# Writing the low half of each weight chunk over its own staging slot, and letting TensorE's use free the slot

## The chip, the cores and the metric

One core of a Trainium2 chip runs the whole program. The metric is the device time of one execution, in microseconds (us). Three runs of the kernel before gave a median of 2979.61 us, the lowest 2978.82 and the highest 2984.75.

## What is computed

The reference is a stack of transformer blocks on 256 tokens of width 1024, in float32. Two layers of a first block come first, each with a gated feed-forward network (FFN, inner width 2816), a mixer of three attention branches, and a second such FFN. Two layers of a second block follow, each with an attention and a mixture of 16 experts of which every token takes two. Every layer modulates its input with vectors computed from a conditioning vector `c`:

```python
c_act = jax.nn.silu(c)
for l in range(DEPTH):
    mod = (c_act @ ada_w[l] + ada_b[l]).reshape(bsz, N_SUB, 3, D_MODEL)[:, :, :, None, :]
    h = modulate(x, norm_pre[l, 0], mod[:, 0, 0], mod[:, 0, 1])
    x = residual_add(x, swiglu(h, ffn_w_gate[l, 0], ffn_w_up[l, 0], ffn_w_down[l, 0]), norm_post[l, 0], mod[:, 0, 2], 0.5)
    ...
```

The product `c_act @ ada_w` is a vector times a very wide matrix. The kernel calls this the modulation, and reads its weights (`ada_stream`) in slices.

## The kernel before

**Weights.** All weights of the matrix products are one stream of 432 chunks of 128 partitions x 2048 float32 (1 MB each), in the order in which TensorE uses them. To keep float32 accuracy, a weight chunk is split into a high half in a rounded type (`w_hi`) and the rest (`w_lo`). Each product is then three matmuls (`mm3`, L1564 to L1571): high by high, high by low, low by high. Three engines and a queue work on a chunk in turn:

- SyncE (the SP queue) loads chunk n into staging slot n mod 6 (`chunk`, L392). It first waits until the low half of chunk n-6 has been written, by the semaphore `chunk_ready`, because VectorE's subtraction is the last reader of the slot.
- ScalarE copies the slot to `w_hi`, buffer n mod 3 (`hi`, L504). It waits for the landing and for TensorE to have finished chunk n-3 (`pe_used`).
- VectorE subtracts, `w_lo` = `stage` - `w_hi`, into a low buffer of its own, n mod 3 (`lo`, L876), and raises `chunk_ready`.
- TensorE waits for `chunk_ready` (`chunk_wait`, L1573), does its matmuls and raises `pe_used`. That semaphore starts at 3 (`PARTS`), so the value n+1 says that chunk n-3 is finished.

**Modulation.** The modulation weights are cut into 40 units of 4 slices (768 KB a slice, one buffer for each of the four slice numbers). SP loads a slice (`ada_slice`, L399) after VectorE has used up the same slice of the unit before. VectorE multiplies and adds each slice in two steps (`ada_add`, L949 to L967, 8 steps a unit), and TensorE then sums the unit over partitions (`sum_unit`, L1642 to L1650). Four units are done at the start of the program, and nine in each of the four dense FFNs (33 chunks each, starting at chunks 0, 71, 104 and 175).

**The dense FFN's block.** An FFN has 11 blocks of 3 chunks. In block g TensorE does chunk 3g-1 (up), a transpose of the hidden values, the sum of a modulation unit, chunk 3g (up), chunk 3g+1 (down). Chunk 3g-1 also waits for `silu(g-1)` of VectorE, which frees the result banks `gu`. VectorE's order in block g is written out by hand (L1036 to L1057); `add` is `ada_add` of the unit of block g:

```python
add(0)
lo(n0 + 3 * g - 1, i)
add(1)
silu(g - 1, i)
add(2)
lo(n0 + 3 * g, i)
...
```

It goes on with add 3, `lo` of chunk 3g+1, add 4, `turn_lo(g-1)`, which the down chunk 3g+1 needs, and adds 5 to 7. Steps 0, 2, 4 and 6 are each the first use of a slice.

**SP's order.** SP executes its waits and issues in program order. In the FFN's loop, chunks and slices are interleaved (L434 to L439):

```python
for a in range(2):
    for q in range(SLICES):
        if q < 3:
            chunk(n0 + 12 + 3 * a + q, i)
        ada_slice(unit_base[k] + 1 + a, q, i)
```

Counted in blocks: slices 0, 1 and 2 of block g's unit stand right behind chunks 3g+3, 3g+4 and 3g+5, and slice 3 behind slice 2. This holds for g = 3 to 10. The four slices of block 2's unit are issued before, in one go.

**The mixture of experts** uses 96 chunks in each of its two layers, with 12 matmuls of 128 x 512 a chunk, where a dense chunk has 24. It loads no slices.

Of the kernel before, what the change touches and what calls it, by code (L numbers as in the profile page):

```python
# [2 lines left out]

# [4 lines left out]
F32 = mybir.dt.float32  # L28
# [6 lines left out]
P = 128  # L35
# [19 lines left out]
CW = 2048  # L55
# [171 lines left out]
def build(nc, wstream, ada_stream, xin, const_in, vec_in, bgate_in, lam_in, rbias_in, t5_in, t5hot_in, rel_in, rw_in, out):  # L227
# [8 lines left out]
    with ExitStack() as ctx:  # L236
# [4 lines left out]
            return ctx.enter_context(nc.semaphore(name))  # L241


        stage = sb("stage", [P, STAGES, CW])
        w_hi = sb("w_hi", [P, PARTS, CW], F32R)
        w_lo = sb("w_lo", [P, PARTS, CW], F32R)

        x = sb("x_tok", [P, NT, D])
        tok = sb("tok", [P, NT, D])
# [140 lines left out]
        @block.sync  # L390
        def _(sp):
            def chunk(n, i=0, rounds=1):  # L392
                if not isinstance(i, int) or n >= STAGES:

                    sp.wait_ge(chunk_ready, n + 1 - STAGES + STAGES * rounds * i)
                at = bass.ds(n + STAGES * rounds * i, 1)
                sp.dma_start(stage[:, n % STAGES, :], wstream[at].rearrange("a p c -> (a p) c")).then_inc(
                    landed[n % STAGES], 16)

            def ada_slice(unit, q, i=0):  # L400

                m = SLICES * unit + q
                if not isinstance(i, int) or m >= SLICES:
                    sp.wait_ge(slice_sum, m + 1 - SLICES + 2 * SLICES * i)
                at = bass.ds(m + 2 * SLICES * i, 1)
                sp.dma_start(ada_stage[:, q, :], ada_stream[at].rearrange("a p c -> (a p) c")).then_inc(
                    ada_landed[q], 16)

            def stream(n, end):

                turns = (end - n) // STAGES
                if turns > 1:
                    with sp.Fori(0, turns) as i:
                        for s in range(STAGES):
                            chunk(n + s, i)
                    n += turns * STAGES
                for m in range(n, end):
                    chunk(m)

            for unit in range(FIRST_UNITS + 1):  # L420
                for q in range(SLICES):
                    ada_slice(unit, q)
                    if unit >= FIRST_UNITS - 1 and q % 4 < 3:
                        chunk(3 * (unit - FIRST_UNITS + 1) + q)
            n = STAGES
            for k, n0 in dense_steps:
                stream(n, n0 + 8)
                if k:

                    sp.wait_ge(x_ready, NT * k)  # L430
                    for q in range(SLICES):
                        ada_slice(unit_base[k], q)
                stream(n0 + 8, n0 + 12)
                with sp.Fori(0, (FFN_UNITS - 1) // 2) as i:  # L434
# [5 lines that stand above are left out]
                n = n0 + 12 + 3 * (FFN_UNITS - 1)  # L440
            stream(n, n_chunks)
            sp.wait_ge(x_ready, NT * NSUB)
            sp.dma_start(out.rearrange("(t p) d -> p t d", p=P), x[:]).then_inc(st_out, 16)
            sp.wait_ge(st_out, 16)
# [420 lines left out]
        def _(dve):  # L865
# [10 lines left out]
            def lo(n, i=0, rounds=1):  # L876

                dve.wait_ge(hi_ready, n + 1 + STAGES * rounds * i)
                dve.tensor_tensor(w_lo[:, n % PARTS, :], stage[:, n % STAGES, :], w_hi[:, n % PARTS, :].bitcast(F32),  # L879
                                  ALU.subtract).then_inc(chunk_ready, 1)  # L880

            def ahead(n):
# [681 lines left out]
        def _(pe):  # L1564
# [11 lines left out]
            def columns(n, dst, k0, kts, first, last, width=512, src=(hT_hi, hT_lo), i=0, pitch=512):  # L1576

                chunk_wait(n, i)
                s = n % PARTS
                for t in range(NT):  # L1580
                    for k in range(kts):
                        c = slice(k * pitch, k * pitch + width)
                        lhs = [v[:, k0 + k, t * P:(t + 1) * P] for v in src]
                        ins = mm3(dst(t), lhs[0], lhs[1], w_hi[:, s, c], w_lo[:, s, c], first and k == 0, last and k == kts - 1)
                ins.then_inc(pe_used, 1)

            def rows(n, lhs, first, last, i=0, rounds=1):

                chunk_wait(n, i, rounds)
                s = n % PARTS  # L1590
                for t in range(NT):
                    for k in range(2):
                        l_hi, l_lo = lhs(k, t)
                        for h in range(2):
                            c = slice(k * D + h * 512, k * D + (h + 1) * 512)
                            ins = mm3(acc[:, 2 * t + h, :], l_hi, l_lo, w_hi[:, s, c], w_lo[:, s, c],
                                      first and k == 0, last and k == 1)
                    if last and t == 0:
                        ins.then_inc(half_done, 1)
                ins.then_inc(pe_used, 1)  # L1600
# [73 lines left out]
            def moe(b, l):  # L1674
# [39 lines left out]
                def up(e, j, half, i=0):  # L1714
                    p, n = e // 2, moe_up_at(n0, e, j) + half
                    if half == 0:
                        if e % 2 == 0 and j == 0:
                            taken(("g", p, KT - 1), i)
                        if not isinstance(i, int) or e:
                            pe.wait_ge(hid_ready, g0 + 2 * e + j - 1 + 8 * i)  # L1720
                    chunk_wait(n, i, 4)
                    slots = slice((e % 2) * P, (e % 2 + 1) * P)
                    src_hi, src_lo = gathered[p % 2]
                    for k in range(4):
                        c = slice(k * 512, (k + 1) * 512)
                        ins = mm3(gu[:, j, :], src_hi[:, 4 * half + k, slots], src_lo[:, 4 * half + k, slots],
                                  w_hi[:, n % PARTS, c], w_lo[:, n % PARTS, c], half == 0 and k == 0, half == 1 and k == 3)
                    ins.then_inc(pe_used, 1)

                def turn_hidden(e, i=0):  # L1730
# [6 lines left out]
                def down(e, h, i=0):  # L1737

                    if h == 0:
                        taken(("hid", e), i)  # L1740
                    n = moe_down_at(n0, e, h)
                    dst = bank(("y", e, h), i)
                    chunk_wait(n, i, 4)
                    for k in range(4):
                        c = slice(k * 512, (k + 1) * 512)
                        ins = mm3(dst, hid_hi[:, k * P:(k + 1) * P], hid_lo[:, k * P:(k + 1) * P],
                                  w_hi[:, n % PARTS, c], w_lo[:, n % PARTS, c], k == 0, k == 3,
                                  signal=pe_used if h and k == 0 else None)
                    ins.then_inc(tr_full, 1)

# [61 lines left out]
            def moe_dense(b):  # L1812
# [14 lines left out]
                def down(e, h, i=0):  # L1827
# [5 lines left out]
                    for t in range(NT):  # L1833
                        for k in range(4):
                            c = slice(k * 512, (k + 1) * 512)
                            ins = mm3(acc[:, 2 * t + h, :], yT_hi[:, k, t * P:(t + 1) * P], yT_lo[:, k, t * P:(t + 1) * P],
                                      w_hi[:, n % PARTS, c], w_lo[:, n % PARTS, c], first and k == 0, last and k == 3)
                        if last and h == 1 and t == 0:
                            ins.then_inc(half_done, 1)
                    ins.then_inc(pe_used, 1)  # L1840
# [49 lines left out]
            for step, b in plan:  # L1890
# [150 lines left out]
                elif kind == "mla_up":  # L2041
# [2 lines left out]
                    pe.wait_ge(o_free, b["ov"])  # L2044
                    wide = acc[:].rearrange("p (t a) c -> p t a c", t=NT)
                    chunk_wait(n)
                    s = n % PARTS
                    for t in range(NT):
                        for h, w in ((0, 512), (1, 256)):
                            for k in range(2):  # L2050
                                c = slice(k * 768 + h * 512, k * 768 + h * 512 + w)
                                ins = mm3(wide[:, t, h, 0:w], yT_hi[:, k, t * P:(t + 1) * P], yT_lo[:, k, t * P:(t + 1) * P],
                                          w_hi[:, s, c], w_lo[:, s, c], k == 0, k == 1)
                    ins.then_inc(pe_used, 1)
                    chunk_wait(n + 1)
                    s = (n + 1) % PARTS
                    pe.wait_ge(ev_ready, b["ev"] + 1)
                    for t in range(NT):
                        for h in range(2):
                            c = slice(h * 512, h * 512 + 512)  # L2060
                            ins = mm3(wide[:, t, h, :], yT_hi[:, 2, t * P:(t + 1) * P], yT_lo[:, 2, t * P:(t + 1) * P],
                                      w_hi[:, s, c], w_lo[:, s, c], True, True)
                    ins.then_inc(pe_used, 1)
                elif kind == "merge":
                    pe.wait_ge(o_free, b["ov"])
# [222 lines left out]
```

## Time and profile before

| what | value |
|---|---|
| median of three runs | 2979.61 us |
| the profiled execution: span from first to last instruction | 2981.6 us |
| TensorE (PE) busy | 2593.6 us, 87% |
| VectorE (DVE) busy | 1984.8 us, 67% |
| ScalarE (ACT) busy | 1269.8 us, 43% |
| mean granted clock of TensorE | 0.892 |
| DMA | 591.74 MB, mean 198 GB/s |

The profile gives the time of each instruction group, who ended an engine's idle time, and the granted clock as a share of 2.4 GHz (1.00 or 0.50). The span of the profiled execution is 2.0 us over the median of the runs; the profile has no other time for that execution than this span, so sums below are made against 2981.6 us and put on the median.

### The profile page before, as it was taken

The numbers are of one execution on the slowest core, as the hardware profiler recorded it, in microseconds if no ns is written. First come the engines' busy times: TensorE is split into PE (matmuls) and PEld (weight loads), VectorE is DVE, ScalarE is ACT, GpSimd is POOL, SyncE is SP. The second block draws the span as 40 slices with busy tenths as digits, with TensorE's granted clock in tenths as the row PEclk, the third lists the DMA queues.
The fourth block names the chain that finished last, engine by engine and source line by source line (L and its number), as shares of the span: only waits on it lengthen the run. The fifth ranks groups of instructions, "written<-read, shape, count | busy, mean of one in ns | idle before, by whom it ended". The sixth has DMA issues, their size and how long they took to land.

```text
span 2981.6 us, 33031 instructions
## 1 busy us (share of the span) xinstructions
PE 2593.6 (87%) x11582; PEld 2113.7 (71%) x11582; DVE 1984.8 (67%) x2444; ACT 1269.8 (43%) x1403; POOL 98.0 (3%) x136
## 2 busy tenths in 40 slices
PE   2998976988998999769989988689999779799997
PEld 2787865866877877658768875478887557578885
DVE  6687354556876874445668856678887444588885
ACT  1333443433333334444333342256666322366663
POOL 1000000000000000000000002000000021000000
PEclk9999956998998999668989998899999785899998
DMA  9585400445875864103458743147777333177773
GB/s 358 231 350 222 169 29 29 162 168 204 357 284 215 356 275 155 43 29 131 151 199 340 315 155 78 57 180 285 269 284 278 136 106 27 65 288 276 276 290 116
DMA packets 89959, 591.74 MB, mean 198 GB/s; under 512 B 10616, under 2 KB 10632, under 8 KB 34432
## 3 DMA queue, kind: packets, MB, share of 16 engines
q1 hardware_dynamic: 85520, 579.90, 50.9%
q0 software_dynamic: 2608, 7.31, 2.0%
q10 hardware_dynamic: 1728, 3.15, 0.4%
q8 instruction: 66, 1.08, 0.1%
q14 instruction: 37, 0.30, 0.0%
HBM read 589.25 MB, written 1.06 MB: 198 GB/s over the span
## 4 chain that ended last, share of the span: by engine, by line
PE 77%; DVE 11%; ACT 5%; issue 3%; POOL 2%; DMA 1%; DVEq 0%; ACTq 0%; POOLq 0%
PE gu L1567 11%; PE gu L1570 11%; PE gu L1571 11%; PE acc L1567 7%; PE acc L1570 7%; PE acc L1571 7%; PE tr L1611 4%; PE gu L1865 4%; DVE w_lo L879 3%; PE acc L1865 2%; PE tr L1567 2%; PE tr L1570 2%; PE tr L1571 2%; PE tr L1696 2%; PE tr L1648 1%
## 5 line engine op out<-in xcount | busy, mean ns | idle before, releaser
L879 DVE TENSOR_TENSOR w_lo<-stage,w_hi 128x2048 fp32r<-128x2048 f32 x432 | 984.6, 2287 | 216.9 <-ACT w_hi L508 216.5
L508 ACT ACTIVATE w_hi<-stage 128x2048 fp32r<-128x2048 f32 x432 | 824.4, 1913 | 408.8 <-PE acc L1571 249.5
L1567 PE MATMUL gu<-w_hi,hT_hi 128*128 128x512 f32 x1152 | 466.2, 405 | 19.1 <-DVE pair L1017 14.3
L1570 PE MATMUL gu<-w_lo,hT_hi 128*128 128x512 f32 x1152 | 458.2, 398 | 0.0
L1571 PE MATMUL gu<-w_hi,hT_lo 128*128 128x512 f32 x1152 | 457.3, 397 | 0.0
L966 DVE SCALAR_TENSOR_TENSOR qk<-proj,c_unit,qk 128x768 f32<-128x768 f32 x280 | 284.0, 1014 | 19.7 <-DMA proj<-ada_stream 8.4
L1567 PEld LDWEIGHTS gu<-w_hi,hT_hi 128*128 128x128 f32 x1152 | 222.5, 193 | 67.7 <-DVE pair L1017 17.6
L1571 PEld LDWEIGHTS gu<-w_hi,hT_lo 128*128 128x128 f32 x1152 | 221.7, 192 | 48.4
L1570 PEld LDWEIGHTS gu<-w_lo,hT_hi 128*128 128x128 f32 x1152 | 222.4, 193 | 43.1
L1567 PE MATMUL acc<-w_hi,hT_hi 128*128 128x512 f32 (+1 forms) x544 | 219.0, 402 | 17.0 <-DVE w_lo L879 12.3
L1570 PE MATMUL acc<-w_lo,hT_hi 128*128 128x512 f32 (+1 forms) x544 | 216.9, 399 | 0.0
L1571 PE MATMUL acc<-w_hi,hT_lo 128*128 128x512 f32 (+1 forms) x544 | 215.9, 397 | 0.0
L1567 PE MATMUL acc<-w_hi,yT_hi 128*128 128x512 f32 x472 | 185.2, 392 | 8.5 <-DVE yT_lo L897 4.5
L1611 PE MATMUL tr<-const,tok 128*128 128x128 f32 x336 | 87.5, 421 | 118.7 <-DVE tok L1241 78.3
L1570 PE MATMUL acc<-w_lo,yT_hi 128*128 128x512 f32 x472 | 184.1, 390 | 0.0
L1571 PE MATMUL acc<-w_hi,yT_lo 128*128 128x512 f32 x472 | 184.0, 390 | 0.0
L1611 PEld LDWEIGHTS tr<-const,tok 128*128 128x128 f32 x336 | 63.2, 217 | 148.6 <-DVE tok L1241 82.1
L706 ACT ACTIVATE tok<-tok,nmax 128x128 f32<-128x128 f32 (+1 forms) x128 | 57.1, 447 | 234.5 <-DVE nmax L1209 233.1
L1567 PEld LDWEIGHTS acc<-w_hi,hT_hi 128*128 128x128 f32 x544 | 106.5, 196 | 43.1 <-issue 15.5
L1865 PE MATMUL gu<-qk 64*128 64x128 f32 (+3 forms) x320 | 117.8, 510 | 11.8 <-DVE qk L1320 4.9
L1571 PEld LDWEIGHTS acc<-w_hi,hT_lo 128*128 128x128 f32 x544 | 106.0, 195 | 21.9
L1567 PE MATMUL tr<-w_hi,yT_hi 128*128 128x512 f32 x256 | 104.2, 407 | 19.6 <-DVE w_lo L879 19.6
(233 smaller groups left out, 3724.9 us busy)
## 6 DMA issues: line engine op xcount, KB each, us to landing
stage<-wstream SPq DMA_DIRECT2D x432, 1024.0 KB, 4.8
proj<-ada_stream SPq DMA_DIRECT2D x160, 768.0 KB, 7.6
tf<-bgate_in ACTq DMA_DIRECT2D x12, 256.0 KB, 3.2
proj<-rel_in POOLq DMA_DIRECT2D x16, 128.0 KB, 4.0
const<-const_in POOLq DMA_DIRECT2D x1, 1028.0 KB, 10.6
x_tok<-x_in POOLq DMA_DIRECT2D x1, 1024.0 KB, 14.2
proj<-t_rows POOLq DMA_DIRECT2D x8, 128.0 KB, 4.0
proj<-rel_in POOLq DMA_DIRECT2D x16, 64.0 KB, 3.5
```

Source lines behind the costliest of these rows:

```text
L508: act.activation(w_hi[:, n % PARTS, :], stage[:, n % STAGES, :], ACT.Copy).then_inc(hi_ready, 1)
L706: ins = act.activation(prob[:, s, lo:lo + w], prob[:, s, lo:lo + w], ACT.Exp, bias=nmax[:, s, q:q + 1], accum_out=rsum[:, s, q:q + 1])
L879: dve.tensor_tensor(w_lo[:, n % PARTS, :], stage[:, n % STAGES, :], w_hi[:, n % PARTS, :].bitcast(F32), ALU.subtract).then_inc(chunk_ready, 1)
L966: ins = dve.scalar_tensor_tensor(total, w, c, total, ALU.mult, ALU.add)
L1567: ins = pe.matmul(dst, l_hi, r_hi, start=start, stop=False, skip_group_check=True)
L1570: pe.matmul(dst, l_hi, r_lo, start=False, stop=False, skip_group_check=True)
L1571: return pe.matmul(dst, l_lo, r_hi, start=False, stop=stop, skip_group_check=True)
L1611: ins = pe.transpose(tr[0:rows_, u % 2, j * P:(j + 1) * P], src, ident)
L1648: ins = pe.matmul(tr[:, u % 2, j:j + 1], ada_acc[:, unit % 2, j * P:(j + 1) * P], ones[:, 0:1], start=True, stop=True)
L1696: ins = pe.matmul(dst[:, part * S:(part + 1) * S], h[:, t, r * P:(r + 1) * P], pick[:, t, :], start=(t == 0), stop=(t == NT - 1), skip_gro ...
L1865: return pe.matmul(dst, lhs, rhs, start=start, stop=stop, skip_group_check=True)
```

## The change

The separate tile `w_lo` goes. The name now stands for the staging tile itself, at the same address, in the rounded type, with 6 slots. VectorE's subtraction reads a slot and writes its result over it. TensorE reads the low half from slot n mod 6, so the slot is in use until TensorE has finished the chunk. SP therefore waits on `pe_used` for chunk n-6, where it waited on `chunk_ready` for chunk n-6. The 24 KB per partition of the three low buffers are left unused. Nothing else is changed: the orders of all engines, the three high buffers and all other waits stay.

```diff
+        stage_at = (nc.sbuf_base + 31) // 32 * 32
         stage = sb("stage", [P, STAGES, CW])
         w_hi = sb("w_hi", [P, PARTS, CW], F32R)
-        w_lo = sb("w_lo", [P, PARTS, CW], F32R)
+        w_lo = nc.alloc_sbuf_tensor_at("w_lo", [P, STAGES, CW], F32R, offset=stage_at)
...
             def chunk(n, i=0, rounds=1):
                 if not isinstance(i, int) or n >= STAGES:
 
-                    sp.wait_ge(chunk_ready, n + 1 - STAGES + STAGES * rounds * i)
+                    sp.wait_ge(pe_used, n + 1 - STAGES + PARTS + STAGES * rounds * i)
...
             def lo(n, i=0, rounds=1):
 
                 dve.wait_ge(hi_ready, n + 1 + STAGES * rounds * i)
-                dve.tensor_tensor(w_lo[:, n % PARTS, :], stage[:, n % STAGES, :], w_hi[:, n % PARTS, :].bitcast(F32),
+                dve.tensor_tensor(w_lo[:, n % STAGES, :], stage[:, n % STAGES, :], w_hi[:, n % PARTS, :].bitcast(F32),
                                   ALU.subtract).then_inc(chunk_ready, 1)
...
                 chunk_wait(n, i)
-                s = n % PARTS
+                s, z = n % PARTS, n % STAGES
...
-                        ins = mm3(dst(t), lhs[0], lhs[1], w_hi[:, s, c], w_lo[:, s, c], first and k == 0, last and k == kts - 1)
+                        ins = mm3(dst(t), lhs[0], lhs[1], w_hi[:, s, c], w_lo[:, z, c], first and k == 0, last and k == kts - 1)
```

The other places where TensorE reads `w_lo` change in the same way.

## Rows read from the trace of the kernel before

**Rows 1.** The page's chain that ended last, and its costliest groups

```profile
PE 77%; DVE 11%; ACT 5%; issue 3%; POOL 2%; DMA 1%; DVEq 0%; ACTq 0%; POOLq 0%
...
L879 DVE TENSOR_TENSOR w_lo<-stage,w_hi 128x2048 fp32r<-128x2048 f32 x432 | 984.6, 2287 | 216.9 <-ACT w_hi L508 216.5
```

**Rows 2.** Windows: one dense FFN block, and 338 us of the first mixture of experts

```profile
core 0: us, PE busy (x) PEld busy (x) DVE busy (x) ACT busy (x) POOL busy (x), PEclk, DMA share, GB/s
...
155.60:173.70 18.10, 18.10 (x90) 15.22 (x89) 15.30 (x15) 6.73 (x5) 0.00 (x0) 1.00 0.88 356
...
1962.00:2300.00 338.00, 327.30 (x1582) 270.65 (x1580) 281.19 (x288) 221.51 (x223) 0.00 (x0) 0.99 0.75 280
```

**Rows 3.** Waits of the SP queue: who was waited for, total us, times, longest us

```profile
SPq L397 <- DVE w_lo L879: 2524.0, 426, 116.1
```

**Rows 4.** Timeline of SP: chunks 21 to 23 and the slices of block 6

```profile
162.75 0.33 SPq L397 DMA_DIRECT2D stage<-wstream  x1
163.27 0.33 SPq L406 DMA_DIRECT2D proj<-ada_stream  x1
166.94 0.33 SPq L397 DMA_DIRECT2D stage<-wstream  x1
167.50 0.33 SPq L406 DMA_DIRECT2D proj<-ada_stream  x1
176.37 0.33 SPq L397 DMA_DIRECT2D stage<-wstream  x1
176.91 0.86 SPq L406 DMA_DIRECT2D proj<-ada_stream  x2
```

**Rows 5.** Timeline of VectorE, block 6, from add 0 to turn_lo

```profile
160.29 2.29 DVE L879 TENSOR_TENSOR w_lo<-stage,w_hi 128x2048 fp32r<-128x2048 f32 x1
...
173.26 0.62 DVE L964 TENSOR_SCALAR qk<-proj,c_unit 128x768 f32<-128x768 f32 x1 [0.21 <-DVE qk L966]
173.79 2.29 DVE L879 TENSOR_TENSOR w_lo<-stage,w_hi 128x2048 fp32r<-128x2048 f32 x1
176.00 1.01 DVE L966 SCALAR_TENSOR_TENSOR qk<-proj,c_unit,qk 128x768 f32<-128x768 f32 x1
176.92 0.68 DVE L1017 TENSOR_TENSOR pair<-pair,gu 128x512 f32<-128x512 f32 x1
...
184.81 1.01 DVE L966 SCALAR_TENSOR_TENSOR qk<-proj,c_unit,qk 128x768 f32<-128x768 f32 x1
187.16 0.69 DVE L1022 TENSOR_TENSOR yT_lo<-tr,yT_hi 128x512 fp32r<-128x512 f32 x1 [1.34 <-ACT yT_hi L582]
```

**Rows 6.** Timeline of ScalarE: steps that start as TensorE ends chunks 13, 15, 16

```profile
162.52 1.92 ACT L508 ACTIVATE w_hi<-stage 128x2048 fp32r<-128x2048 f32 x1 [2.96 <-PE acc L1571]
168.40 0.60 ACT L582 ACTIVATE yT_hi<-tr 128x512 fp32r<-128x512 f32 x1 [3.96 <-PE tr L1611]
...
175.28 0.60 ACT L570 ACTIVATE pair<-gu 128x512 f32<-128x512 f32 x1 [4.49 <-PE gu L1571]
...
180.65 1.92 ACT L508 ACTIVATE w_hi<-stage 128x2048 fp32r<-128x2048 f32 x1 [2.95 <-PE acc L1571]
```

**Rows 7.** DMA issues of the page: count, KB each, median us to landing

```profile
stage<-wstream SPq DMA_DIRECT2D x432, 1024.0 KB, 4.8
proj<-ada_stream SPq DMA_DIRECT2D x160, 768.0 KB, 7.6
```

**Rows 8.** Timeline of TensorE, after 3.58 us of idle in the first FFN

```profile
89.45 0.79 PE L1567 MATMUL gu<-w_hi,hT_hi 128*128 128x512 f32 x1 [3.58 <-DVE pair L1017]
90.04 0.63 PE L1570 MATMUL gu<-w_lo,hT_hi 128*128 128x512 f32 x1
90.46 0.63 PE L1571 MATMUL gu<-w_hi,hT_lo 128*128 128x512 f32 x1
...
96.51 0.39 PE L1567 MATMUL gu<-w_hi,hT_hi 128*128 128x512 f32 x1
96.74 0.39 PE L1570 MATMUL gu<-w_lo,hT_hi 128*128 128x512 f32 x1
```

**Rows 9.** Window of the low clock around that restart

```profile
88.80:95.60 6.80, 6.15 (x15) 4.80 (x16) 5.00 (x3) 0.00 (x0) 0.00 (x0) 0.50 0.81 292
```

More of the change, by code:

```diff
@@ L1589, in rows @@
                 chunk_wait(n, i, rounds)
-                s = n % PARTS
+                s, z = n % PARTS, n % STAGES
                 for t in range(NT):
@@ L1595, in rows @@
                             c = slice(k * D + h * 512, k * D + (h + 1) * 512)
-                            ins = mm3(acc[:, 2 * t + h, :], l_hi, l_lo, w_hi[:, s, c], w_lo[:, s, c],
+                            ins = mm3(acc[:, 2 * t + h, :], l_hi, l_lo, w_hi[:, s, c], w_lo[:, z, c],
                                       first and k == 0, last and k == 1)
@@ L1726, in up @@
                         ins = mm3(gu[:, j, :], src_hi[:, 4 * half + k, slots], src_lo[:, 4 * half + k, slots],
-                                  w_hi[:, n % PARTS, c], w_lo[:, n % PARTS, c], half == 0 and k == 0, half == 1 and k == 3)
+                                  w_hi[:, n % PARTS, c], w_lo[:, n % STAGES, c], half == 0 and k == 0, half == 1 and k == 3)
                     ins.then_inc(pe_used, 1)
@@ L1746, in down @@
                         ins = mm3(dst, hid_hi[:, k * P:(k + 1) * P], hid_lo[:, k * P:(k + 1) * P],
-                                  w_hi[:, n % PARTS, c], w_lo[:, n % PARTS, c], k == 0, k == 3,
+                                  w_hi[:, n % PARTS, c], w_lo[:, n % STAGES, c], k == 0, k == 3,
                                   signal=pe_used if h and k == 0 else None)
@@ L1836, in down @@
                             ins = mm3(acc[:, 2 * t + h, :], yT_hi[:, k, t * P:(t + 1) * P], yT_lo[:, k, t * P:(t + 1) * P],
-                                      w_hi[:, n % PARTS, c], w_lo[:, n % PARTS, c], first and k == 0, last and k == 3)
+                                      w_hi[:, n % PARTS, c], w_lo[:, n % STAGES, c], first and k == 0, last and k == 3)
                         if last and h == 1 and t == 0:
@@ L2046, in _ @@
                     chunk_wait(n)
-                    s = n % PARTS
+                    s, z = n % PARTS, n % STAGES
                     for t in range(NT):
@@ L2052, in _ @@
                                 ins = mm3(wide[:, t, h, 0:w], yT_hi[:, k, t * P:(t + 1) * P], yT_lo[:, k, t * P:(t + 1) * P],
-                                          w_hi[:, s, c], w_lo[:, s, c], k == 0, k == 1)
+                                          w_hi[:, s, c], w_lo[:, z, c], k == 0, k == 1)
                     ins.then_inc(pe_used, 1)
                     chunk_wait(n + 1)
-                    s = (n + 1) % PARTS
+                    s, z = (n + 1) % PARTS, (n + 1) % STAGES
                     pe.wait_ge(ev_ready, b["ev"] + 1)
@@ L2061, in _ @@
                             ins = mm3(wide[:, t, h, :], yT_hi[:, 2, t * P:(t + 1) * P], yT_lo[:, 2, t * P:(t + 1) * P],
-                                      w_hi[:, s, c], w_lo[:, s, c], True, True)
+                                      w_hi[:, s, c], w_lo[:, z, c], True, True)
                     ins.then_inc(pe_used, 1)
```

## The prediction

> **What bounds the kernel now.** I read the chain of waits first: TensorE holds 77% of it, VectorE 11%, and DMA 1% [rows 1]. Staging is not a limit. Over the 432 chunks SP waits 2524 us for the low halves [rows 3]: it is always ahead. The windows show what TensorE's neighbours have to spare. A block of a dense FFN takes 18.10 us, TensorE is busy in all of them, VectorE in 15.30, and DMA moves 356 GB/s at a busy share of 0.88 [rows 2]. So there TensorE is the bound, but slices and chunks flow with little slack. I then followed one block on the four timelines, because SP's queue carries two streams and the change alters the wait of only one of them.
>
> **The subtraction in place.** All 432 subtractions stay, with the same operands and sizes, 2287 ns each [rows 1]. I take 0 for the new destination. No row has one in place. If the write over a source made each 1% faster or slower, that would be 10 us of VectorE, on the chain for 11% of its length, so 1 us either way. TensorE reads the same number of values from another address: 0 as well. Removing the three low buffers gives nothing, because nobody waited for them separately: the high buffer's wait for chunk n-3 covers both, and stays.
>
> **The chunk's own load.** A slot now comes free when TensorE ends chunk n-6, not when chunk n-6 has been subtracted. ScalarE's copy of chunk n waits in any case for the end of chunk n-3. The load thus has at least the time of three chunks on TensorE. Matmuls follow each other every 0.23 us [rows 8], so this is 3 x 24 x 0.23 = 16.6 us in dense parts and 3 x 12 x 0.23 = 8.3 us in the experts, against 0.2 us until the issue and 4.8 us to the landing [rows 7]. In the experts the mean is 338 / 92 = 3.7 us a chunk, 11.0 us for three (92 subtractions lie in the window of rows 2). Landings up to 8 us are hidden. I take 0 there too. In the attention stages two fewer chunks are prefetched. Six slots stay full, which is 6 x 24 x 0.23 = 33 us of TensorE work, and the loads that follow start one per chunk used.
>
> **What stands behind the chunk in SP's queue** is where the time goes. In block 6 slice 0 of the modulation stands behind chunk 21, and chunk 21 waits for chunk 15. Before, the subtraction of chunk 15 ended at 160.29 + 2.29 = 162.6, chunk 21 was issued at 162.75 and the slice at 163.27 [rows 4, 5]. VectorE began to use it at 173.26 [rows 5], 10.0 us after the issue, of which the median landing takes 7.6 [rows 7]. After the change the issue waits for the end of chunk 15 on TensorE, which is 175.28 [rows 6]. That is 12.5 us later, and 2 us past the moment of use. VectorE is in order: behind `add(0)` stand the subtraction of chunk 17 and `silu`, both of which TensorE needs for chunk 17.
>
> The late slice now closes a loop through TensorE, so I work out its period, from the start s of chunk 3g-1 to the start of chunk 3g+2:
>
> - s to the end of chunk 3g: chunk 15 ended 12.76 us after chunk 13 (175.28 - 162.52, [rows 6]), with the transpose and the unit's sum in between: 12.8.
> - End of chunk 3g to the issue of slice 0: 0.15 for the chunk (162.75 - 162.6) and 0.5 for the slice [rows 4, 5]: 0.7.
> - Issue to landing: the median is 7.6 [rows 7], with other transfers queued ahead. The DMA will be less crowded. A 1 MB chunk alone takes 4.8. At 356 / 0.88 = 405 GB/s a chunk needs 2.6 us of transfer and a slice 1.9. So a slice issued 0.5 behind a lone chunk lands after 4.8 + 1.9 - 0.5 = 6.2. I take 6.2, with 7.6 as the other end.
> - Landing to the next start: from `add(0)` at 173.26 to the end of `silu` at 177.60 [rows 5], and 0.2 for two semaphores: 4.5.
>
> The sum is 24.2 us, where the block took 18.1: 6.1 more. Part of it is taken inside the block. Slice 2 is issued at the end of chunk 3g-1, 5.4 after s; it lands at 5.4 + 0.7 + 6.2 = 12.3; then add 4 (1.0) and `turn_lo` (0.7) end at 14.2, and the down chunk that waited for them could have begun at 12.8. TensorE thus idles 1.4 us before the down chunk and 4.7 us before chunk 3g+2. This second stall does not lengthen the loop, except once at the FFN's end.
>
> Blocks 3 to 10 are concerned, 8 in each of 4 FFNs. The first loses less, some 5 us, since the block before still ran at the old pace. Per FFN: 5 + 7 x 6.1 + 1.4 = 49; for four FFNs 196 us. The four slices of block 2 stay early: they stand behind the FFN's chunk 7, which waits for chunk 1, and are used after three more chunks, over 16 us later.
>
> **TensorE's clock** adds to that. Before, it was granted 1.00 throughout the blocks [rows 2]. After an idle of 3.58 us matmuls followed each other every 0.43 us instead of 0.23, and the granted clock stood at 0.50 (1.2 GHz) in a window of 6.8 us [rows 8, 9]. About 14 matmuls were slow: 14 x 0.20 = 2.8 us lost. A stall of 4.7 us is longer than that one, so I expect the low clock in most blocks. The lost time lies between s and the end of chunk 3g, so it lengthens the loop in full. Its ends are 0 and 2.8 us a block; I take 2.4, near the only row that has such a stall: 32 x 2.4 = 77 us.
>
> The Trainium skill ("TensorE: Matmul & The Clock Gate", section "HAM oscillation — how this bites in real kernels") describes this pattern: a loop whose matmuls stop for a DMA in each turn starts every turn at the low clock. By that rule every block pays, and the sum is that of the rival "every block cold". The one stall of this trace agrees with it.
>
> **Sum.** 196 + 77 = 273 us over the profiled execution's 2981.6. The median of the runs is 2.0 us less, so I put it on 2979.6: **3253 us**. A difference of 0.2%, 6 us, is about what a measurement of this kernel tells from no change.
>
> **The rivals.**
> - *Every block cold, or crowded landings* (0.2). The low clock costs its full 2.8 us or more in each of the 32 blocks, 196 + 90, or slices take 7.6 us: 31 x 1.4 = 43 us on top. Together 3310. For it: the median of rows 7. Against it: the lighter DMA load of a longer block.
> - *The clock stays up* (0.2). The stall is cut in two and the clock holds: 2980 + 196 = 3176. For it: TensorE is fully busy around the stalls. Against it: rows 8 and 9.
> - *The experts pay as well* (0.05). VectorE is busy for 281 of 338 us there [rows 2], and a load that lands late stops ScalarE, VectorE and TensorE in turn. If each of the 192 chunks lost 0.5 us, it would be 96 us more: 3350. It needs landings above 8 us; the median is 4.8.
> - *The slices come in time: not slower* (0.03). The slack of a slice before was 10.0 - 7.6 = 2.4 us. If SP was held back by less than this, every block would keep 18.1 us and the time would be 2980. It decides at a delay of 2.4 us; rows 4 to 6 show 12.5.
>
> The change surely does what it says: every chunk's wait is replaced.
>
> **How the numbers follow.** The forecast case (low clock in most blocks) has 0.52 and goes from 3200 to 3290. Adding the case of the clock that stays up takes the range down to 3160, the cold and crowded case takes it up to 3330. What is left out are the last two rivals and the tails. Slower by over 0.2%: 0.96; within 0.2%: 0.03; faster: 0.01, for a gain of the writes in place that no row shows.
>
> **What would show it.** In the windows of a dense FFN the block's period is 26 to 27 us instead of 18.1, with VectorE's 15.3 us of work unchanged and DMA down to about 240 GB/s. `add(0)` of VectorE (L964) has idle time ended by DMA `proj<-ada_stream`, about 8 us in a block, where before there was 0.2. TensorE's idle before chunk 3g-1 is ended by `pair` L1017, and the granted clock drops in most blocks. SP waits for PE, not for `w_lo`. The experts take the same 338 us, the attention stages the same time, and L879 the same 2287 ns. The prediction is wrong if slices are used without a wait, if the clock stays at 1.00, or if the time outside the dense FFNs changes by more than 10 us.

## The result, and the profile after

The changed kernel took 3263.99 us (median of 4 runs, 3259.84 to 3272.76), the kernel before 2981.16 us beside it. The ratio is 1.094, with a 95% interval from 1.092 to 1.097. The span of the profiled execution is 3261.9 us, 280.3 more than before. Line numbers of the changed kernel are 19 lower than before: L397 is L378, L406 is L387, L879 is L860, L966 is L947.

The page of the changed kernel: the chain that ended last, and the two groups of VectorE's that matter.

```profile
PE 66%; DVE 13%; DMA 8%; issue 6%; ACT 5%; POOL 1%; SPq 1%; DVEq 0%; ACTq 0%; POOLq 0%
...
L860 DVE TENSOR_TENSOR w_lo<-stage,w_hi 128x2048 fp32r<-128x2048 f32 x432 | 984.5, 2287 | 181.2 <-ACT w_hi L489 180.7
...
L947 DVE SCALAR_TENSOR_TENSOR qk<-proj,c_unit,qk 128x768 f32<-128x768 f32 x280 | 284.4, 1016 | 299.9 <-DMA proj<-ada_stream 288.8
```

DMA went from 1% of the chain to 8%, all of it the slices' landing. VectorE waited 288.8 us for slices in L947, and 107.9 us more in L945, which is `add(0)`. The subtraction costs the same 2287 ns as in [rows 1]: writing in place is free.

The windows of the changed kernel, one dense block and then the first and second experts' stages from the end of their first chunk to the end of their last:

```profile
core 0: us, PE busy (x) PEld busy (x) DVE busy (x) ACT busy (x) POOL busy (x), PEclk, DMA share, GB/s
...
209.90:237.10 27.20, 21.37 (x88) 17.00 (x88) 15.21 (x15) 6.88 (x6) 0.00 (x0) 0.87 0.60 231
...
2246.70:2639.50 392.80, 357.07 (x1681) 293.12 (x1681) 308.96 (x314) 237.36 (x240) 2.39 (x4) 0.96 0.70 257
2884.80:3250.40 365.60, 344.04 (x1634) 283.59 (x1633) 288.70 (x291) 226.73 (x229) 0.00 (x0) 0.98 0.70 258
```

The block that took 18.10 us [rows 2] takes 27.2. VectorE's work in it is the same, 15.2 us, and DMA is down to 231 GB/s. The same stages of the experts took 392.7 and 365.8 us before:

```profile
1963.20:2355.90 392.70, 356.93 (x1681) 293.02 (x1680) 308.93 (x314) 237.51 (x240) 2.40 (x4) 0.96 0.69 257
2604.40:2970.20 365.80, 344.21 (x1634) 283.62 (x1633) 288.68 (x291) 226.91 (x229) 0.00 (x0) 0.98 0.68 253
```

Their 192 chunks lost nothing. Where the difference lies, by the ends of TensorE's chunks: from the end of the first to the end of the last chunk, each dense FFN took 200.1 us before, and 271.8, 274.3, 273.5 and 273.6 us after. That is 1093.2 against 800.4, 293 more. All the rest of the program is 12.5 us shorter (280.3 - 292.8).

More than half of the 12.5 us lies right behind the four FFNs, from the end of their last chunk to the end of the next chunk of the stream: 21.7 to 21.8 us before, 19.9 after, 7.4 in all. The windows of the first, in the kernel before and in the changed kernel:

```profile
278.90:300.70 21.80, 11.68 (x42) 9.17 (x43) 15.35 (x21) 7.71 (x11) 3.71 (x7) 0.69 0.23 89
```

```profile
353.20:373.10 19.90, 9.56 (x41) 7.77 (x42) 15.27 (x21) 7.75 (x11) 3.73 (x7) 0.74 0.13 53
```

TensorE idles 8.76 us there before and 8.74 after, then does transposes and the next chunk. That chunk began with matmuls 0.43 us apart before and 0.23 us apart after: the clock was back at 1.00 earlier in the changed kernel. The attentions of the second block gave 3.6 and 3.3 us (more on them at e9 to e11), and the program's first chunk ended 2.7 us later.

One turn of the loop, on three engines. The first is SP, from the end of chunk 13 on. It issues chunks 19 to 21, with slices 1 to 3 of block 5's unit and slice 0 of block 6's:

```profile
184.40 0.33 SPq L378 DMA_DIRECT2D stage<-wstream  x1
184.99 0.33 SPq L387 DMA_DIRECT2D proj<-ada_stream  x1
194.69 0.33 SPq L378 DMA_DIRECT2D stage<-wstream  x1
195.28 0.86 SPq L387 DMA_DIRECT2D proj<-ada_stream  x2
201.93 0.33 SPq L378 DMA_DIRECT2D stage<-wstream  x1
202.46 0.33 SPq L387 DMA_DIRECT2D proj<-ada_stream  x1
```

Then VectorE, which uses those slices:

```profile
191.23 1.02 DVE L947 SCALAR_TENSOR_TENSOR qk<-proj,c_unit,qk 128x768 f32<-128x768 f32 x1 [4.18 <-DMA proj<-ada_stream]
...
201.54 1.02 DVE L947 SCALAR_TENSOR_TENSOR qk<-proj,c_unit,qk 128x768 f32<-128x768 f32 x1 [3.96 <-DMA proj<-ada_stream]
202.48 0.68 DVE L1003 TENSOR_TENSOR yT_lo<-tr,yT_hi 128x512 fp32r<-128x512 f32 x1
...
208.69 0.62 DVE L945 TENSOR_SCALAR qk<-proj,c_unit 128x768 f32<-128x768 f32 x1 [2.21 <-DMA proj<-ada_stream]
209.23 2.28 DVE L860 TENSOR_TENSOR w_lo<-stage,w_hi 128x2048 fp32r<-128x2048 f32 x1
211.43 1.01 DVE L947 SCALAR_TENSOR_TENSOR qk<-proj,c_unit,qk 128x768 f32<-128x768 f32 x1
212.36 0.68 DVE L998 TENSOR_TENSOR pair<-pair,gu 128x512 f32<-128x512 f32 x1
```

And TensorE's restart one block later:

```profile
240.51 0.79 PE L1548 MATMUL gu<-w_hi,hT_hi 128*128 128x512 f32 x1 [4.44 <-DVE pair L998]
...
241.95 0.63 PE L1548 MATMUL gu<-w_hi,hT_hi 128*128 128x512 f32 x1
...
243.23 0.63 PE L1548 MATMUL gu<-w_hi,hT_hi 128*128 128x512 f32 x1
...
246.66 0.40 PE L1548 MATMUL gu<-w_hi,hT_hi 128*128 128x512 f32 x1
...
247.35 0.39 PE L1548 MATMUL gu<-w_hi,hT_hi 128*128 128x512 f32 x1
```

Slice 0 of block 6's unit is issued at 202.46, right behind chunk 21, which waited for TensorE, and VectorE starts on it at 208.69, 6.2 us later. The end of `silu` is at 213.04. One block later TensorE restarts after 4.44 us of idle, with matmuls of one kind 1.28 us apart (241.95 to 243.23) where at full clock they are 0.69 apart (246.66 to 247.35; every third matmul stands here). In [rows 4, 5] the same slice had waited for VectorE; now VectorE waits for it, and for the slices of L947 too.

### The profile page after: what moved, and what is told of

It is laid out like the page before. It is cut to its first block, busy times and chain, and to the rows that moved or that the text cites. A ratio compares the mean times of both kernels' runs of the same rounds, so it can differ in the third digit from the quotient of the medians.

```text
span 3261.9 us, 32833 instructions
## 1 busy us (share of the span) xinstructions
PE 2675.4 (82%) x11582; PEld 2154.7 (66%) x11582; DVE 1983.7 (61%) x2444; ACT 1268.8 (39%) x1403; POOL 97.8 (3%) x136
## 4 chain that ended last, share of the span: by engine, by line
PE 66%; DVE 13%; DMA 8%; issue 6%; ACT 5%; POOL 1%; SPq 1%; DVEq 0%; ACTq 0%; POOLq 0%
PE gu L1548 11%; PE gu L1551 10%; PE gu L1552 10%; DMA proj<-ada_stream 8%; PE acc L1548 5%; PE acc L1551 5%; PE acc L1552 5%; PE tr L1592 4%; DVE w_lo L860 3%; PE gu L1846 3%; PE acc L1846 2%; PE tr L1548 2%; PE tr L1551 2%; PE tr L1552 2%; DVE qk L947 1%
## 5 line engine op out<-in xcount | busy, mean ns | idle before, releaser
L860 DVE TENSOR_TENSOR w_lo<-stage,w_hi 128x2048 fp32r<-128x2048 f32 x432 | 984.5, 2287 | 181.2 <-ACT w_hi L489 180.7
L1548 PE MATMUL gu<-w_hi,hT_hi 128*128 128x512 f32 x1152 | 498.7, 433 | 167.2 <-DVE pair L998 162.0
L1551 PE MATMUL gu<-w_lo,hT_hi 128*128 128x512 f32 x1152 | 484.4, 420 | 0.0
L1552 PE MATMUL gu<-w_hi,hT_lo 128*128 128x512 f32 x1152 | 481.5, 418 | 0.0
L947 DVE SCALAR_TENSOR_TENSOR qk<-proj,c_unit,qk 128x768 f32<-128x768 f32 x280 | 284.4, 1016 | 299.9 <-DMA proj<-ada_stream 288.8
L1548 PEld LDWEIGHTS gu<-w_hi,hT_hi 128*128 128x128 f32 x1152 | 239.8, 208 | 234.2 <-issue 161.0
L1552 PEld LDWEIGHTS gu<-w_hi,hT_lo 128*128 128x128 f32 x1152 | 237.0, 206 | 55.1
L1551 PEld LDWEIGHTS gu<-w_lo,hT_hi 128*128 128x128 f32 x1152 | 239.2, 208 | 47.5
L1548 PE MATMUL acc<-w_hi,hT_hi 128*128 128x512 f32 (+1 forms) x544 | 216.8, 399 | 17.4 <-DVE w_lo L860 12.3
L563 ACT ACTIVATE yT_hi<-tr 128x512 fp32r<-128x512 f32 x44 | 26.3, 597 | 428.7 <-PE tr L1592 428.7
L1548 PEld LDWEIGHTS acc<-w_hi,yT_hi 128*128 128x128 f32 x472 | 91.1, 193 | 93.3 <-issue 69.0
## 6 DMA issues: line engine op xcount, KB each, us to landing
x_tok<-x_in POOLq DMA_DIRECT2D x1, 1024.0 KB, 15.2
```

The source lines that it names most:

```text
L563: act.activation(hid_hi, tr[:, u % 2, :], ACT.Copy).then_inc(th_ready, 1)
L860: dve.tensor_tensor(w_lo[:, n % STAGES, :], stage[:, n % STAGES, :], w_hi[:, n % PARTS, :].bitcast(F32), ALU.subtract).then_inc(chunk_read ...
L947: ins = dve.scalar_tensor_tensor(total, w, c, total, ALU.mult, ALU.add)
L1548: ins = pe.matmul(dst, l_hi, r_hi, start=start, stop=False, skip_group_check=True)
L1551: pe.matmul(dst, l_hi, r_lo, start=False, stop=False, skip_group_check=True)
L1552: return pe.matmul(dst, l_lo, r_hi, start=False, stop=stop, skip_group_check=True)
```

## The experiments

All are short edits of one of the two kernels. "Early" is this edit of SP's order, which puts a slice behind a chunk that is three places ahead in the stream:

```diff
-                stream(n0 + 8, n0 + 12)
+                stream(n0 + 8, n0 + 9)
...
-                                chunk(n0 + 12 + 3 * a + q, i)
+                                chunk(n0 + 9 + 3 * a + q, i)
...
-                n = n0 + 12 + 3 * (FFN_UNITS - 1)
+                n = n0 + 9 + 3 * (FFN_UNITS - 1)
```

| run | kernel | median us | ratio to before, 95% interval |
|---|---|---|---|
| changed | in place, wait for TensorE | 3263.99 | 1.092 to 1.097 |
| e1 | changed, early | 2975.32 | 0.9956 to 0.9979 |
| e2 | before, wait for TensorE | 3263.52 | 1.092 to 1.097 |
| e3 | before, wait for TensorE outside the loop | 2990.50 | 1.0014 to 1.0043 |
| e4 | changed, slices one chunk earlier | 2975.55 | 0.9961 to 0.9989 |
| e5 | changed, filler matmuls | 3220.38 | 1.076 to 1.083 |
| e6 | e1 with six high buffers | 2954.64 | 0.9904 to 0.9938 |
| e7 | before, early | 2984.19 | 1.0003 to 1.0033 |
| e8 | changed, slices issued by GpSimd | 2975.83 | 0.9981 to 1.0000 |
| e9 | e2, early | 2975.74 | 0.9959 to 0.9985 |
| e10 | e7 again | 2985.86 | 0.9989 to 1.0019 |
| e11 | e1 again | 2975.38 | 0.9953 to 0.9977 |

The kernel before had medians of 2982.38 us beside e1 to e4, 2979.69 beside e5 to e8 and 2982.92 beside e9 to e11.

**e1: the changed kernel with the slices early.** What was expected:

> The changed kernel, with the slices of a modulation unit standing one group of three chunks earlier in SP's queue (slice 0 of block g's unit behind chunk 3g, not 3g+3). The low half stays in place and every chunk still waits for TensorE. Theory (the loss is the slices' wait behind a chunk in SP's queue): a slice is then issued at least 12 us before VectorE needs it, the block takes 18.1 us and the time is 2981, within 10. Rival A (the shared slot or the write in place is slow by itself): 3264, unchanged. Rival B (two fewer chunks are loaded ahead, and that starves TensorE): 3264 or close to it, as the chunks' own issues don't move.

Measured: 2975.32 us. Both rivals fall. The low half still lies in the staging slot and every chunk still waits for TensorE, so neither the shared slot nor the shorter prefetch costs time. One block in the windows of e1, and VectorE's first use of a slice in it:

```profile
156.40:174.50 18.10, 18.10 (x89) 15.24 (x88) 15.36 (x14) 6.73 (x5) 0.00 (x0) 1.00 0.98 373
```

```profile
174.57 0.62 DVE L945 TENSOR_SCALAR qk<-proj,c_unit 128x768 f32<-128x768 f32 x1 [0.22 <-DVE qk L947]
```

The block is back at 18.10 us and VectorE no longer waits for a DMA.

**e2: the wait alone, in the kernel before.**

```diff
-                    sp.wait_ge(chunk_ready, n + 1 - STAGES + STAGES * rounds * i)
+                    sp.wait_ge(pe_used, n + 1 - STAGES + PARTS + STAGES * rounds * i)
```

> The kernel before with one edit: SP waits for TensorE's end of chunk n-6 instead of the subtraction of chunk n-6. The low half keeps its three buffers of its own. Theory: 3264, within 5, as the wait is the whole loss. Rival A (write in place or shared slot): 2981.

Measured: 3263.52 us, 0.5 from the changed kernel. The wait is the whole loss and the write in place has no part in it.

**e3: the wait everywhere but in the loop.**

```diff
+                    if loop:
+                        sp.wait_ge(chunk_ready, n + 1 - STAGES + STAGES * rounds * i)
+                    else:
+                        sp.wait_ge(pe_used, n + 1 - STAGES + PARTS + STAGES * rounds * i)
```

> The kernel before, with SP's wait for TensorE on all chunks except the 24 chunks of each dense FFN's loop among which the slices stand (those wait for the subtraction, as before; low halves in buffers of their own). Theory: 336 of 432 chunks wait for TensorE and nothing is lost: 2981, within 6. Rival B (fewer chunks ahead costs everywhere, the experts above all): 3000 to 3100.

Measured: 2990.50 us, 8 over the 2982.38 beside it; the expectation of 2981 within 6 missed. Rival B's low end of 3000 is not reached. The trace tells where the 8 come from. Each FFN took 204.4 to 204.9 us instead of 200.1, 18 in all, while the blocks in mid-loop took the usual 18.1 us. The rest of the program was 11 us shorter. At an FFN's start chunk n0+11 stands ahead of the loop in SP's queue and waits for TensorE here, and slice 0 of block 3 stands two issues behind it: it went out at 116.73 us in e3 and at 109.56 before. VectorE's first use of that slice in e3, whose line numbers are 3 higher than before:

```profile
124.83 0.62 DVE L967 TENSOR_SCALAR qk<-proj,c_unit 128x768 f32<-128x768 f32 x1 [4.57 <-DMA proj<-ada_stream]
```

One late slice per FFN, 4.57 us: the mechanism of the loop, once. In the experts, where 192 chunks wait for TensorE, the two stages took 392.7 and 365.7 us.

**e4: the slices one chunk earlier.** In the changed kernel the numbers 9 of the early edit are 11.

> The changed kernel with the slices only one chunk earlier in SP's queue (slice 0 of block g's unit behind chunk 3g+2). By the theory's loop slice 0 is issued when chunk 3g-4 ends, 7.2 us earlier than in the changed kernel (one chunk of 5.4 us, the transpose and the sum), the loop closes in 24.2 - 7.2 = 17.0 us, under the 18.1 us that TensorE needs, and the stall before the down chunk goes as slice 2 comes 5.4 us earlier: 2985, from 2980 to 3000. Were the loss only proportional to the delay (10 us of 12.5), a third to a half of it would stay: 3080 to 3160.

Measured: 2975.55 us, under the 2980 to 3000 that was expected. In the medians, moving the slices by one chunk in SP's queue takes away as much as moving them by three. In the profiled execution the FFNs still took 201.6 to 203.6 us, 9 more in sum than in e1, in the first three turns of the loop (up to 20.6 us); the later turns took 18.1 to 18.3. The loss is not proportional to the delay: it is there when the loop through SP, DMA, VectorE and TensorE is longer than TensorE's own work, and all but gone when it is shorter. The end of chunk 3g-4 took the place of the end of chunk 3g-3 in it.

**e5: filler matmuls in the stall.**

```diff
                     down(n0 + 3 * g + 1, g - 1, isinstance(i, int) and g == 1, False, i)
+                    if g >= 2:
+                        for _ in range(18):
+                            pe.matmul(tr[:, u_of(g - 1) % 2, :], hT_hi[:, 0, 0:P],
+                                      hT_hi[:, 0:2, :].rearrange("p a s -> p (a s)"), start=True, stop=True)
```

> The changed kernel plus 18 matmuls of 128x512 without use in every dense FFN block from the second on, right behind the down chunk, where TensorE idles some 4.5 us (40 blocks in all, of which 36 lie in blocks 3 to 10 or close to them; 18 x 0.23 = 4.1 us each). They write a bank that is free there and change no result. Theory (part of the loss is the low clock after each stall): the clock stays at 1.00 in the loop, the block falls from 27.0 to 24.5 us, and the time is 3264 - 32 x 2.5 = 3184, from 3175 to 3205, although work was added. Rival (the low clock lies off the loop, or the stall is not idle time that can be filled): 3264 or more, up to 3264 + 36 x 4.1 = 3410.

Measured: 3220.38 us. The kernel does 648 more matmuls and is 44 us faster than the changed kernel, where the rival had it slower. Two of its blocks in the windows:

```profile
175.00:199.90 24.90, 22.80 (x106) 18.47 (x106) 14.87 (x14) 5.64 (x6) 0.00 (x0) 1.00 0.63 247
199.90:224.80 24.90, 22.80 (x106) 18.47 (x106) 15.70 (x16) 7.31 (x6) 0.00 (x0) 1.00 0.67 255
```

In these two blocks the granted clock stands at 1.00 and the block at 24.9 us, 2.3 under the changed kernel's 27.2. Over the last seven turns of all four FFNs the mean is 25.0 us against 27.2; the first turn or two of each FFN still had some low clock. The expectation of 3184 (3175 to 3205) missed, by my count of the fillers. Seven periods per FFN lie between two stalls, which gives 7 x 2.2 = 15 us; the filler of block 10 has no stall to fill and adds 4.1. That leaves 11 per FFN, and the FFNs took 264.3, 261.4, 261.9 and 261.2 us, which is 7.5 to 12.9 less than in the changed kernel and 44 in sum. That this sum equals the difference of the medians is chance: the four runs lie between 3206.80 and 3228.30 us and the profiled one is the slowest of them, its span is only 35.4 us shorter than the changed kernel's, and outside the FFNs it took 9 us more (e9 to e11 come back to this).

**e6: six high buffers in the freed memory.** `PARTS = 6` in e1, one line; ScalarE's copy of chunk n then waits for chunk n-6.

> The kernel of e1 (in place, slices early) with six high buffers instead of three, which takes the 24 KB per partition that the change freed. ScalarE's copy then waits for chunk n-6, not n-3. Theory: the copies stand in a fixed order among ScalarE's other steps and TensorE is the bound in the FFNs and the experts, so little is gained: 2960 to 2981. If the three high buffers hold back the start of stages, more: 2930 to 2960.

Measured: 2954.64 us, the fastest version: 0.9921 of the kernel before, interval 0.9904 to 0.9938. This is under the 2960 to 2981 of the theory and in the range of the other case. It beats both kernels, and it uses what the change brings, the 24 KB per partition. The experts' two stages in e6:

```profile
1946.20:2332.70 386.50, 355.30 (x1682) 291.92 (x1681) 310.19 (x315) 237.52 (x241) 2.40 (x4) 0.96 0.71 261
2578.10:2937.10 359.00, 341.99 (x1634) 281.86 (x1633) 288.50 (x291) 225.10 (x229) 0.00 (x0) 0.98 0.71 263
```

They are 6.3 and 6.7 us shorter than in e1 (392.8 and 365.7), mostly in steps of 0.65 us in every second expert. That is 13.0 of the 27.6 us between the spans of the two profiled executions (2976.1 and 2948.5; the medians are 20.7 apart). The FFNs give 4.5, and the rest lies between the stages. Which wait the three more buffers take away was not traced further.

**e7: the kernel before, with the slices early.**

> The kernel before (three low buffers, SP waits for the subtraction) with the slices three chunks earlier in SP's queue, as in e1. A slice had 2.4 us to spare there already, so nothing is gained: 2981, within 6. It is the fair partner of e1: the difference between the two is what writing in place costs when the slices don't hang on it, expected 0 within 6 us.

Measured: 2984.19 us. Early slices alone gain nothing, as said. But e1, which differs in the wait and in the place of the low half, was 9 us faster, where no difference within 6 was expected. This led to e9 to e11.

**e8: the slices on GpSimd's queue.** In the changed kernel SP's loop issues only the chunks, and GpSimd issues the slices of the FFNs, each after its wait on `slice_sum`, with semaphores of their own for the landing.

```diff
+                elif kind == "ffn" and not step[3]:
+                    ...
+                            pool.wait_ge(slice_sum, m + 1 - SLICES)
+                            pool.dma_start(ada_stage[:, q, :], ada_stream[m:m + 1].rearrange("a p c -> (a p) c")).then_inc(
+                                ada_pool[q], 16)
```

> The changed kernel with the FFNs' slices issued by GpSimd, which is idle there, each after VectorE's use of the same slice of the unit before; SP keeps the chunks alone, in unchanged order and with their wait for TensorE. Theory (two streams in one in-order queue): the slices no longer stand behind a chunk, 2981 to 3000 (GpSimd's issues may cost more). Rival (the slices are late because the DMA engines are busy with other transfers, or VectorE frees them late): above 3150.

Measured: 2975.83 us, as fast as e1 and under the 2981 to 3000 that was expected, with SP's order of the chunks untouched. The rival falls: it was the queue, neither the DMA engines nor VectorE's release of the slices.

**e9 to e11: the 9 us between e1 and e7.** e9 is e2 with the early edit; e10 and e11 are the kernels of e7 and e1 once more, on the same chip.

> The kernel before, low halves in three buffers of their own, with two edits: SP waits for TensorE's end of chunk n-6 (as in e2) and the slices stand three chunks earlier (as in e1). It differs from e1 only in that the low half isn't written in place, and from e7 only in SP's wait. If the 7 to 9 us by which e1 beats e7 come from the later loads (in the last attention but one they no longer meet GpSimd's bias loads), this gives e1's time, 2975 within 4. If they come from writing in place, it gives e7's, 2984.

> The kernel of e7 once more, on the same chip as e9: before, with slices early and the wait for the subtraction. Where the later loads are the cause: 8 us over e9, with the stage between chunks 219 and 220 at 92 us or more, against 88.2 in e9. Otherwise the same as e9.

> The kernel of e1 once more, on the same chip as e9 and e10: the time of e9, within 3 us, if writing in place is free.

Measured: 2975.74, 2985.86 and 2975.38 us. The low half's place makes no difference (e9 against e11), SP's wait makes one of 10 us (e9 against e10). The stretch between the ends of chunks 219 and 220, with the first attention of the second block in it, in the kernel before, in e9, in e10 and in e11:

```profile
1804.30:1896.20 91.90, 63.61 (x273) 43.98 (x274) 65.42 (x147) 27.91 (x74) 17.27 (x19) 0.80 0.23 40
```

```profile
1803.40:1891.70 88.30, 60.94 (x274) 42.06 (x274) 65.14 (x147) 27.92 (x74) 17.28 (x19) 0.83 0.22 30
```

```profile
1805.00:1902.80 97.80, 69.42 (x273) 48.03 (x274) 65.42 (x147) 27.91 (x74) 17.28 (x19) 0.76 0.22 38
```

```profile
1799.30:1887.50 88.20, 60.87 (x273) 42.04 (x274) 65.13 (x147) 27.91 (x74) 17.25 (x19) 0.83 0.22 30
```

The kernels that wait for the subtraction move more in this stretch (40 and 38 GB/s, against 30) and run it at a lower clock. The profiled execution of e10 is the slowest of its twelve (2994.45 us, median 2985.86), so its 97.8 can't be set against the 10 us between the medians. What they move is two chunks, in the middle of the attention, seen on the timelines of SP, GpSimd and TensorE of the kernel before:

```profile
1824.65 2.53 SPq L397 DMA_DIRECT2D stage<-wstream  x2
```

```profile
1826.87 1.07 POOL L496 DMA_DIRECT2D proj<-t_rows  x2 [14.92 <-PE gu L1865]
```

```profile
1834.42 0.76 PE L1865 MATMUL gu<-qk 64*128 64x128 f32 x2 [2.06 <-DMA proj<-t_rows]
```

The bias loads of GpSimd run beside the two chunks, and TensorE then waits 2.06 us for a bias. With the wait for TensorE, one chunk of the two is loaded at the start of the stretch and the other only after it. That the wait for the bias then sets off the lower clock is argued from the order of these rows; no run took the bias wait away by itself. In the next attention (2415.7 to 2604.4 before) TensorE waits 2.6 us for a bias in the kernel before and for none in the changed kernel, and the stretch takes 188.7 us against 185.4.

One trace speaks against the two chunks as the whole cause. In e5 SP waits for TensorE, no chunk is loaded in mid-attention and TensorE waits for no bias, and still the same stretch took 95.3 us, at a clock of 0.73:

```profile
2049.00:2144.30 95.30, 70.17 (x273) 47.54 (x274) 65.54 (x147) 27.89 (x74) 17.23 (x19) 0.73 0.21 28
```

So this stretch can fall to the lower clock without them. What the runs show is that SP's wait makes the difference between the medians; by which way stays open.

## Why the prediction was right

The forecast was 3253 us in a range of 3160 to 3330; 3264 was measured. By its steps:

- **The subtraction in place costs 0.** Shown: 2287 ns before and after, e2 equals the changed kernel, e9 equals e11.
- **The chunk's own load costs 0.** Shown for the experts (392.7 and 365.8 us before, 392.8 and 365.6 after) and by e1 for the dense blocks. The second half of the step was off: I took 0 for the attention stages, and the program outside the FFNs became 12.5 us shorter. The prediction called itself wrong if that time changed by more than 10 us, so this sign of being wrong came true. Of the 12.5 us, 6.9 lie in the two attentions of the second block, where e9 and e10 show that SP's wait makes a difference of about 10 us. Another 7.4 lie behind the FFNs, in the matmuls after an idle. The wait alone does not bring them: e1, e9 and e11 have it and took 21.6 to 21.8 us there. e3, e4, e6 and e8 took the shorter time behind one to three of their FFNs; what decides it is not shown. A gain was not among my bounds.
- **The slices behind the chunks.** Shown: e2 brings the whole loss by the wait alone, e1, e4 and e8 take all of it away, or nearly, by SP's order or queue alone. The rival "the slices come in time" was decided at a delay of 2.4 us, and VectorE's waits show that it was passed. Where VectorE would wait was off: about 8 us a block were named for `add(0)`, and the trace's waits give 107.9 / 32 = 3.4 us there and 288.8 / 32 = 9.0 us at the later slices.
- **The loop's terms.** Issue to landing was taken as 6.2 and was 6.2 (202.46 to 208.69; the page's median is 6.3). End of chunk to issue 0.7, and landing to the next start 4.5, are confirmed within 0.2 by the rows above. The stall before chunk 3g+2 was 4.1 to 5.0 us in most turns where 4.7 was expected, the one before the down chunk 1.4 to 1.6 where 1.4 was. (The working of that 1.4 has 14.2 where its terms give 12.3 + 1.0 + 0.7 = 14.0; 0.2 for semaphores is left unsaid.)
- **The clock.** Expected 2.4 us a block, and that was right. Each of the 32 turns has a stretch at 0.50, and by the starts of its matmuls (0.43 us apart instead of 0.23) the low clock cost 1.5 to 3.3 us a turn, about 2.5 on average; e5, with the clock up in most turns, has a mean period 2.2 us shorter. Here the trace agrees with the rule of the Trainium skill that I weighed ("TensorE: Matmul & The Clock Gate", section "HAM oscillation — how this bites in real kernels"): each turn starts cold. So of the rival "every block cold, or crowded landings" the first half came about, at a little less than its 2.8 us, and the second did not.
- **The size.** The FFNs lost 293 us, where the terms summed to 273. The first turn of each loop took 26.4 us on average, 8.3 over 18.1, where 5 and 2.4 had been taken: 4 x 0.9 = 4 us. The 28 turns behind it took 27.2 us where 24.2 + 2.4 = 26.6 had been taken: 28 x 0.6 = 17 us. How the 0.6 is shared between the loop and the clock the traces don't tell. The 12.5 us won outside the FFNs, which I had not foreseen, hid most of the miss. That the forecast came within 11 us is in part luck: two misses of opposite sign.

## What to carry to other kernels

When a wait is made later, list what stands behind it on the same in-order queue: here the loads that waited had 11.6 us to spare in the dense blocks (by the prediction's terms, 16.6 - 0.2 - 4.8), and the loads of another stream behind them had 2.4. A late load costs nothing until the path from its issue through its user and back to its release is longer than the bound engine's work, and then it sets the period of every turn, with the restart at a low clock on top. If the order of the queue is moved with the wait, the change is free, and the memory that it frees can be spent: six high buffers gave 2955 us against 2980 to 2983.

## What was not expected

- Matmuls added to a stall made the kernel faster: 648 of them gave 44 us back between the medians, and in two blocks of the loop the granted clock stood at 1.00, where one of the changed kernel's had 0.87.
- Loading weights further ahead came with a loss. With two chunks of 1 MB loaded in mid-attention beside small bias loads, the stretch took 91.9 or 97.8 us instead of 88.3. In the two kernels of the same queue wait (before and e10) the same stretch came out 5.9 us apart, with granted clocks of 0.80 and 0.76, and e5 had 95.3 us at 0.73 without those loads. How much of the loss is theirs is not shown.
- The same work behind an FFN took two times, by when the clock came back: 21.7 to 21.8 us behind all four in the kernel before and in e1, 19.9 to 20.0 behind all four in the changed kernel and in e2.
- The SP queue waited longer in sum than any engine in both kernels, 2524.0 us before. Its total said nothing on whether something behind the wait was late: the chunk waits of the changed kernel sum to 2832.4 us.
